# First up slab by token tiles, made ready during the gates, and start modulation chunks moved forward

## What is computed

```python
mod_l = silu_c @ w_mod[l] + b_mod[l]                    # first block, 3 x 1024 columns, two streams
h_l = rmsnorm(x, norm_g[l]) * (1 + sc_l[:, None]) + sh_l[:, None]
f_in, f_gate, q_a, kv_a, k_pe, m_gate = split_cols(h_l @ w_in, EVEN_SPLITS)

ada = (cond_act @ w_ada + b_ada)[:, None, :]            # second block, 6 x 1024 columns
sh1, sc1, g1, sh2, sc2, g2 = jnp.split(ada, 6, axis=-1)
...
gates = jax.nn.sigmoid(gate_logit)
for n in range(N_BRANCH):
    term = gates[..., n * D_MODEL:(n + 1) * D_MODEL] * (branches[n] @ w_branch[n])
    merged = term if merged is None else merged + term
mixed = merged @ w_o
x = layer_norm(ALPHA * x + g1 * mixed) * ln1_g + ln1_b
u2 = layer_norm(x) * (1 + sc2) + sh2
hdn = jnp.square(jax.nn.relu(u2 @ w_up + b_up))         # 4096 hidden features
x = layer_norm(ALPHA * x + g2 * (hdn @ w_down)) * ln2_g + ln2_b
```

## Time and profile before

| | |
|---|---|
| median of 3 runs | 1402.86 us (1402.53 to 1403.52) |
| the profiled execution | 1406.7 us, span of its instructions 1404.9 us |
| PE busy | 1324.1 us, 94% |
| DVE, ACT, POOL busy | 949.1 us (68%), 501.4 us (36%), 151.7 us (11%) |
| DMA | 257.96 MB, mean 184 GB/s |
| mean granted clock of PE | 0.987 |

### The profile page before, as it was taken

The page is one execution under the profiler, slowest core; times in us unless marked ns, Lnnn a source line. Parts: engine busy times, 40 slices in busy tenths (PEclk is TensorE's granted clock), DMA queues, the critical chain, the costliest instruction groups (busy, mean ns, idle before and its releaser), DMA issues.

```text
span 1404.9 us, 19098 instructions
## 1 busy us (share of the span) xinstructions
PE 1324.1 (94%) x7963; PEld 1091.0 (78%) x7963; DVE 949.1 (68%) x1215; ACT 501.4 (36%) x756; POOL 151.7 (11%) x168
## 2 busy tenths in 40 slices
PE   5899999999999899999998999999999999999996
PEld 3689756546875459889987889886989988889895
DVE  4658857656558566587788766667667778755546
ACT  3322025404246124533323333433354333343432
POOL 2111110000000010012222000001001231100000
PEclk9999999999999999999999999999999999999999
DMA  9553551115330355576774666554556776355551
GB/s 359 181 168 117 188 199 71 61 60 180 123 133 1 139 192 202 195 270 242 292 274 147 234 228 225 197 177 176 189 190 249 261 279 215 124 188 195 182 180 60
DMA packets 104911, 257.96 MB, mean 184 GB/s; under 512 B 8214, under 2 KB 11767, under 8 KB 104571
## 3 DMA queue, kind: packets, MB, share of 16 engines
q1 hardware_dynamic: 80432, 171.75, 35.9%
q0 software_dynamic: 20192, 75.58, 14.8%
q10 hardware_dynamic: 4202, 9.42, 2.0%
HBM read 255.68 MB, written 1.05 MB: 183 GB/s over the span
## 4 chain that ended last, share of the span: by engine, by line
PE 72%; DVE 15%; ACT 4%; DMA 4%; issue 3%; POOL 1%; ACTq 1%; POOLq 0%; SPq 0%; DVEq 0%
PE bank L764 69%; DMA weight_ring<-in_w_in_dram 2%; DVE weights_low L2127 2%; PE bank L924 2%; DMA start_ring<-in_w_mod_dram 1%; ACT weights_high L1560 1%; ACT odd_prob L1741 1%; DVE negated_maxima L2361 1%; DVE statistics L2081 1%; POOL inverse_roots L663 1%; ACT even_A L1686 1%; DVE modulation_sums L1969 1%; DVE x L2080 1%; DVE even_A L2066 1%; DVE xn L2074 1%
## 5 line engine op out<-in xcount | busy, mean ns | idle before, releaser
L2127 DVE TENSOR_TENSOR weights_low<-weight_ring,weights_high 128x2048 fp32r<-128x2048 f32 (+1 forms) x124 | 272.5, 2200 | 230.8 <-ACT weights_high L1560 230.7
L1560 ACT ACTIVATE weights_high<-weight_ring 128x2048 fp32r<-128x2048 f32 (+1 forms) x124 | 227.5, 1837 | 395.5 <-PE bank L764 297.0
L764 PE MATMUL bank<-uT_high,weights_high 128*128 128x256 f32 (+1 forms) x1200 | 341.5, 285 | 8.5 <-issue 2.9
L764 PE MATMUL bank<-uT_low,weights_high 128*128 128x256 f32 (+1 forms) x1200 | 339.4, 283 | 0.0
L764 PE MATMUL bank<-uT_high,weights_low 128*128 128x256 f32 (+1 forms) x1200 | 339.3, 283 | 0.0
L764 PEld LDWEIGHTS bank<-uT_high,weights_high 128*128 128x128 f32 (+1 forms) x1200 | 228.4, 190 | 14.2 <-ACT gate_tanh L1882 7.4
L764 PEld LDWEIGHTS bank<-uT_low,weights_high 128*128 128x128 f32 (+1 forms) x1200 | 228.5, 190 | 1.1
L764 PEld LDWEIGHTS bank<-uT_high,weights_low 128*128 128x128 f32 (+1 forms) x1200 | 228.4, 190 | 0.5
L1969 DVE SCALAR_TENSOR_TENSOR modulation_sums<-modulation_ring,silu_c_columns,modulation_sums 128x1024 f32<-128x1024 f32 x112 | 148.7, 1327 | 17.9 <-DMA modulation_ring<-in_w_ada_dram 9.8
L764 PE MATMUL bank<-weights_high,hidden_high 128*128 128x512 f32 x256 | 102.5, 400 | 3.3 <-DVE weights_low L2127 3.3
L764 PE MATMUL bank<-weights_low,hidden_high 128*128 128x512 f32 x256 | 101.7, 397 | 0.0
(11 more groups left out here) (303 smaller groups left out, 2199.2 us busy)
## 6 DMA issues: line engine op xcount, KB each, us to landing
weight_ring<-in_w_in_dram SPq DMA_DIRECT2D x52, 1024.0 KB, 6.6
modulation_ring<-in_w_ada_dram POOLq DMA_DIRECT2D x48, 1024.0 KB, 7.2
weight_ring<-in_w_up_dram SPq DMA_DIRECT2D x32, 1024.0 KB, 5.4
weight_ring<-in_w_down_dram SPq DMA_DIRECT2D x32, 1024.0 KB, 5.0
modulation_ring<-in_w_mod_dram POOLq DMA_DIRECT2D x16, 1024.0 KB, 5.5
weight_ring<-in_o_w_in_dram SPq DMA_DIRECT2D x10, 1024.0 KB, 5.3
weight_ring<-in_w_branch_dram SPq DMA_DIRECT2D x16, 512.0 KB, 3.8
weight_ring<-in_w_o_dram SPq DMA_DIRECT2D x8, 1024.0 KB, 7.5
```

The costliest lines, as they stand in the source:

```text
L764: return track(pe.matmul(*args, **kw))
L1560: act.activation(ring[:, s, c0:kn * cols], wring[:, slot, c0:kn * cols], ACT.Copy).then_inc(S["high_ready"], 1)
L2127: dve.tensor_tensor(lo[:, s, c0:kn * cols], wring[:, slot, c0:kn * cols], hi[:, s, c0:kn * cols].bitcast(F32), ALU.subtract).then_inc(w_fr ...
```

## The change

**Layers of the second block.** The two slabs of `up0` move forward in `LAYER_SLABS`, one ahead of `branch5` and one ahead of `branch6`. They leave the two-slot rings of parts: ACT's `high_late` and DVE's `low_late` write their parts into `hidden_high` and `hidden_low` (not yet in use) and into two new tiles that lie over the queries, keys and values. Behind `o1`, PE turns `xn` tile by tile, ACT modulates and DVE splits blocks of 4 x 128 features of one token tile (`split_block`), and `up0` is multiplied with 128 tokens out and 512 hidden features as columns (`up_of_tile`); ACT copies that out and PE turns it back (`turn_up`) into the banks of `up0`, the second tile's part after the first half of `up1`. DVE's order in `residual_of_mixed` changes, and two of its steps stand before ACT's and DVE's parts of `o1` 1. The number of fillers goes from 10 to 12. POOL makes the roots in the order 0, 2, 1, 3.

**Start.** The row products of chunks 4 and 5 move ahead of the second half of the transposes, those of 6 and 7 behind the first k step of `fin`, and the quarters behind the first and second k step. ACT's copies follow. The fillers there go from 8 to 3.

```diff
                + [s for j in range(8) for s in halves(f"gate{j}") + [(f"branch{j}", 0)]]
-               + halves("o0", "o1", "up0") + ...
+               + [s for j in range(8) for s in halves(f"gate{j}") + [("up0", j - 5)] * (j in (5, 6)) + [(f"branch{j}", 0)]]
+               + halves("o0", "o1") + ...
...
# POOL
-                    tile_roots(1, range(4))
+                    tile_roots(1)
# PE, start
             for c in range(PE_MODS):
                 add_quarters(c, 0)
+            start_rows(4, 5)
             turn_x("xT", xn_e, range(4, KD), TALL)
-            keep_busy(fin[0], 8)
+            keep_busy(fin[0], 3)
...
                     if half == 0 and k == 0:
-                        start_rows(4)
+                        start_rows(6, 7)
+                        add_quarters(0, 1)
                     if half == 0 and k == 1:
-                        start_rows(5, 6)
-                    if half == 0 and k == 2:
-                        add_quarters(0, 1)
-                        start_rows(7)
+                        add_quarters(1, 1)
-                if half == 0:
-                    add_quarters(1, 1)
# PE, behind o1
                 reduce_part(1)
-                keep_busy(start(("x2T", 0)), 3)
                 reduce_part(2)
-                keep_busy(start(("x2T", 0)), 3)
-                turn_xn("x2T", TC, between=lambda: reduce_part(3))
-                keep_busy(start(("up", 0, 0)), 4)
+                keep_busy(start(("x2T", 0, 0)), 2)
+                turn_tile(0, "x2T", TC)
+                reduce_part(3)
+                keep_busy(start(("x2T", 1, 0)), 10)
...
+                o = start(("upt", 0))
+                up_of_tile(o, 0, range(6))
+                turn_tile(1, "x2T", TC)
+                up_of_tile(o, 0, range(6, KD))
+                o = start(("upt", 1))
+                up_of_tile(o, 1, range(4))
+                firsts_up = [start(("up", 0, i)) for i in range(2)]
+                turn_up(firsts_up, 0)
+                up_of_tile(o, 1, range(4, KD))
+                def finish_first(k):
+                    if k == 4:
+                        turn_up(firsts_up, 1)
# ACT
+                def high_late(h):
+                    slot, before = sec.slab(("up0", h))
+                    copied(("PV", 3))
+                    act.wait_ge(w_full[slot], before * 16 + 16)
+                    act.activation(up_parts[h][0], wring[:, slot, :], ACT.Copy).then_inc(S["late_high"], 1)
...
+                    if g in (5, 6):
+                        high_late(g - 5)
                     if g < 7:
                         high(f"gate{g + 1}")
                         gate_tanh(g)
...
-                high("o1", "up0")
+                high("o1", "up1")
# DVE
+                def low_late(h):
+                    slot, _ = sec.slab(("up0", h))
+                    hi, lo = up_parts[h]
+                    dve.wait_ge(S["late_high"], sec.at("late_high", h + 1))
+                    dve.tensor_tensor(lo, wring[:, slot, :], hi.bitcast(F32), ALU.subtract).then_inc(w_free[slot], 1)
...
+                    if g in (5, 6):
+                        low_late(g - 5)
                     if g < 7:
                         low(f"gate{g + 1}")
...
                 def residual_of_mixed(m):
+                    link(halves_of_tile("o", 1, 0))
                     link(halves_of_tile("o", 0, 1))
                     variance(0, False, LN_EPS)
                     centred(0)
+                    link(scaled(0, m))
+                    statistics_again(0)
+                    mod_columns(1, mcol2, 0)
+                    mod_columns(2, mcol2, 1)
                     link(halves_of_tile("o", 1, 1))
                     variance(1, False, LN_EPS)
-                    link(scaled(0, m))
-                    statistics_again(0)
+                    normal(0, m + 1)
                     centred(1)
-                    normal(0, m + 2)
-                    scaled(1, m + 1).then_inc(S["norm1"], 1)
+                    scaled(1, m + 2).then_inc(S["norm1"], 1)
                     dve.wait_ge(S["norm1"], sec.at("norm1", 1))
+                    split_block("x2T", 0, 0)
                     statistics_again(1)
-                    mod_columns(1, mcol2, 0)
-                    mod_columns(2, mcol2, 1)
+                    split_block("x2T", 0, 1)
                     normal(1, m + 3)
```

147 lines of the change are left out of this document (81 added, 66 removed).

## The result

The changed kernel takes 1431.49 us (median of 4 runs, 1430.27 to 1434.65), the kernel before 1403.19 beside it. The ratio is 1.0211, with a 95% interval of 1.0195 to 1.0227: 27 to 32 us slower, more than the 12 that were forecast and outside the range. One of the four runs of the kernel before was in a slower state (1488.13 us), and the ratio leaves it out. The profiled execution has a span of 1430.5 us against 1404.9, 25.6 more, so its rows account for nearly all of the loss (the kernel before was profiled in an execution of 1406.7 us, some 4 above its median).

The account below looks back on a forecast made before the run. PE was taken to bound the kernel, 72% of the span. -9.0 + 10.3 + 8.5 + 0.9 + 0.7 = +11.4, plus 1 us for half clock, on the median 1402.86 gave 1415 us; range 1402 to 1423.

Parts of the forecast that it names:

- The sign: Whole kernel: slower, 1415 us against a median of 1402.86; slower was given 0.78.
- the three mechanisms: Start gains 9.0 us; gates 6 and 7 start late, 10.3 and 8.5; behind o1 down0 comes 0.9 and 0.7 later.
- the 1 that was allowed: 1 us added to the sum of +11.4 for half clock after the new stalls.
- Start, -9.0: Start: PE's 3.88 us wait in fin and the clock's fall go; 9.0 us gained, 5.8 if the clock fell anyway.
- I let the whole gain through: Behind the start: DVE and DMA work is tied to PE's progress, so all 9.0 us were kept.
- Gates, +10.3 and +8.5: Gates 5 to 7: gate6 1 and gate7 1 wait for DVE's subtractions of up0; 10.3 us in layer 0, 8.5 in layer 1.
- the chain of layer 0: Gates, layer 0: up0 0 lands, is converted and subtracted, then gate6 1 loads; gate 6 4.7 us late, 10.3 by gate 7.
- the slabs fit in: Rival at the gates: gate6 1 and gate7 1 land before ACT needs them, 1395 us, faster; chance 0.12.
- a fall in gate 7: Clock rival: half clock behind gate 7's stall is not covered, +3.3 us per layer, 1421 us; chance 0.25.
- the row of 54 us: Start of the kernel before: clock 0.50 after the 3.88 us wait; cited for the bound of 2.5 us lost behind o1.
- Behind `o1`, +0.9 and +0.7: From o1 to down0: up0 by token tiles makes down0 start 0.9 us later in layer 0, 0.7 in layer 1.
- the fillers' overrun: Behind o1: 10 fillers after g2's reduction, 4.1 us, overrun the wait for the first split by 3 us.

Follow-up runs that it names:

- start_alone: The kernel before with only the start part added (row products of chunks 4 to 7, quarters, 3 fillers): 1394.82 us, ratio 0.9925.
- own_place: The changed kernel with the two up0 slabs loaded outside the ring of three, at the same moment and with the same bytes: 1431.95 us, ratio 1.0193.

## Why the prediction was wrong

The sign, the three mechanisms and their places were right. The size was wrong: -9.0 + 10.3 + 8.5 + 0.9 + 0.7 + 1 = +12.4 us against 25.6 in the trace. Of the 13.2 us that are missing, the start has 2.3 (0.3 in itself, 2.0 given back), the chains of the gates 2.3 and 3.5, the clock in gate 7 1.9 beyond the 1 that was allowed, and the stretch behind `o1` 2.7 and 2.5; the stretches for which nothing was forecast return 1.8.

**Start, -9.0.** Right in itself (-8.7), with every step as forecast: chunks 4 and 5 there in time, `fin` at 33.3, no wait, clock 1.00. The step that failed is "I let the whole gain through": 2.3 us were given back at 130 to 141 us, 0.7 in a wait behind DVE and a modulation chunk and 1.6 in the clock behind it. Another 1.3 went at 456 us, again in the clock, and about as much came back between the two, so that 6.7 are left at gate 5. The first loss is one of nine traces in fifteen, as start_alone's section says: how much of the gain a run keeps is partly luck.

**Gates, +10.3 and +8.5.** Measured from gate 5's start, the chain of layer 0 reads, forecast then trace: landing 5.4, 5.5; ACT's conversion 1.9, 1.9; DVE done with its chunks at 8.0, 8.1; subtraction 2.29, 3.27; landing of `gate6` 1 6.5, 6.6; gate 6 at 20.5, 21.4. Then `gate7` 1 6.5, 8.15. So two terms were mis-sized. The subtraction of `up0` 0 started while POOL's two adds still ran (670.43 to 674.10) and took 1.0 longer; the second landing was 1.65 longer. In layer 1 the subtraction takes 3.27 again and the landings 7.8 and 8.2 for 6.5. Why the landings vary, no run singles out. The subtraction hangs on the rule of the Trainium skill that the prediction weighed (GPSIMD Engine Reference, 8. Key points): POOL contends for SBUF interfaces with DVE instructions that have two SBUF inputs. The trace agrees with it, 3.27 us beside POOL's adds and 2.29 without; I had gone by 2.29.

The chain was right, but not the whole cause. The prediction had the DMA engines done in time and put the late slab down to the ring; own_place shows that the queue of bytes alone gives nearly the same stall. The forecast held against "the slabs fit in" that only a much earlier free slot could help; own_place gives that slot, and the slab is late all the same.

**Clock.** This is the term that was mis-sized most. The sum allowed 1 us; "a fall in gate 7" was left to a rival at 0.25. It was there in both layers (1.5 and 1.4, the fall in gate 6 being covered as said), it was in the transposes and g2's matmuls behind `o1` (4.9 us in layer 0 and 4.8 in layer 1 for the 2.7 of the sum), and in the give-back at 135 us (1.6). That is some 9 us, the largest single miss. The rival also priced it too high for one gate (3.3) and did not look behind `o1`, although the sum bounded it there by the row of 54 us. A row of the kernel before could have warned: the forecast cites that the clock held behind the wait of 2.71 us in layer 0, but in layer 1 it fell behind a wait of the same length (0.59 from 1203 to 1206 us), and transposes and g2's matmuls took 4.3 us there. The Trainium skill's rule beside the rival (TensorE: Matmul & The Clock Gate, HAM oscillation) fits the four late gates, where PE waits for a slab: behind 6.23, 4.94, 7.44 and 5.07 us of idling the clock was 0.50 to 0.60 each time. For the shorter waits the rows give no such rule, as the last section shows.

**Behind o1, +0.9 and +0.7.** Became +3.6 and +3.2. Transposes 7.1 us after the first reduction (forecast 7.2) and `down0` 16.05 us into `up1` (forecast 16.1) were right, the fillers' overrun too; 2.2 of the 2.6 us by which `down0` missed its forecast in layer 0, and 2.1 of 2.5 in layer 1, are the clock above. That both the fillers and DVE's order were worth undoing (7.5 and 2.2 us) was in the terms, unused.

## What to carry to other kernels

A slab brought forward costs twice: its bytes stand ahead of the slab that is needed next, and its slot comes back only when the last engine has read it. Find both times before the first experiment; where they tie, undoing one shows next to nothing. Load early, but behind what is due sooner and outside a ring that is full, and price a new wait with the matmuls that may run at half clock behind it, not by its idle time alone: here these were 1.4 to 2.2 us each.
